# All weight products 256 columns wide, with each streamed operand 192 bytes past its stationary one modulo 256

## What is computed

```python
# first block: ff1, mixer (stick-breaking attention and a gated MLP), ff2
x = x + 0.5 * (silu(h @ w_gate) * (h @ w_up)) @ w_down          # h = rmsnorm(x), width 2816
proj = h @ w_in                                                  # 1024 -> 7168
merged = g_a * (y_a @ w_branch_a) + g_b * (y_b @ w_branch_b)
x = x + merged @ w_out
x = x + 0.5 * (silu(h @ w_gate) * (h @ w_up)) @ w_down
# second block: MoBA layer, then FoX layer, each followed by a squared-ReLU MLP of width 4096
h = h + attention(rms_norm(h) @ w_qkv) @ w_o
h = h + square(relu(rms_norm(h) @ w_up)) @ w_down
```

## Time and profile before

| | |
|---|---|
| median of three runs | 1222.33 us |
| profiled execution | 1222.73 us, its span 1221.0 us |
| PE busy / weight loads | 1209.9 us (99%) / 1033.0 us (85%), 6823 each |
| VectorE busy | 851.5 us (70%) |
| ScalarE busy | 627.8 us (51%) |
| DMA | 221.74 MB, 182 GB/s over the span |
| granted TensorE clock | 0.998 of full |

### The profile page before, as it was taken

The page is one execution under the profiler, slowest core; times in us unless marked ns, Lnnn a source line. Parts: engine busy times, 40 slices in busy tenths (PEclk is TensorE's granted clock), DMA queues, the critical chain, the costliest instruction groups (busy, mean ns, idle before and its releaser), DMA issues.

```text
span 1221.0 us, 17603 instructions
## 1 busy us (share of the span) xinstructions
PE 1209.9 (99%) x6823; PEld 1033.0 (85%) x6823; DVE 851.5 (70%) x1309; ACT 627.8 (51%) x965; POOL 90.2 (7%) x192
## 2 busy tenths in 40 slices
PE   9999999999999999999999999999999999999998
PEld 8788888898888888888888988888888888888886
DVE  6877767576575668777776767865756676876754
ACT  6544446566544446444456665544447465744443
POOL 2000000121000010000003210000000540000000
PEclk9999999999999999999999999999999999999999
DMA  7766666545754555655565445866553654676640
GB/s 235 226 195 199 196 196 192 177 137 161 253 199 146 173 156 183 220 179 185 193 199 171 125 143 183 275 191 191 189 171 110 176 165 156 208 249 192 192 141 35
DMA packets 174899, 221.74 MB, mean 182 GB/s; under 512 B 9268, under 2 KB 103568, under 8 KB 174816
## 3 DMA queue, kind: packets, MB, share of 16 engines
q1 hardware_dynamic: 173264, 217.09, 56.2%
q0 software_dynamic: 1248, 3.00, 0.9%
q10 hardware_dynamic: 304, 0.53, 0.1%
HBM read 219.52 MB, written 1.06 MB: 181 GB/s over the span
## 4 chain that ended last, share of the span: by engine, by line
PE 96%; DVE 1%; DMA 1%; ACT 1%; issue 0%; SPq 0%; DVEq 0%; ACTq 0%
PE bank L1478 56%; PE bank L1565 22%; PE bank L1572 11%; PE bank L1499 1%; PE bank L1738 1%; PE bank L1721 1%; DMA raw<-in_ff_w_up 1%; PE bank L1698 1%; PE bank L1696 1%; PE bank L1712 0%; DVE w_lo L980 0%; PE bank L1742 0%; PE bank L1689 0%; DVE work L1034 0%; PE bank L1930 0%
## 5 line engine op out<-in xcount | busy, mean ns | idle before, releaser
L980 DVE TENSOR_TENSOR w_lo<-raw,w_hi 128x1024 fp32r<-128x1024 f32 (+1 forms) x448 | 490.9, 1119 | 199.2 <-ACT w_hi L628 198.9
L628 ACT ACTIVATE w_hi<-raw 128x1024 fp32r<-128x1024 f32 (+1 forms) x448 | 422.2, 972 | 274.4 <-PE bank L1572 137.1
L1565 PE MATMUL bank<-xt,w_hi 128*128 128x512 f32 x1216 | 320.8, 396 | 2.7 <-DVE work L1034 1.9
L1565 PEld LDWEIGHTS bank<-xt,w_hi 128*128 128x128 f32 x1216 | 213.9, 188 | 40.6 <-DVE work L1034 1.8
L1572 PEld LDWEIGHTS bank<-xt,w_lo 128*128 128x128 f32 x1216 | 167.6, 188 | 16.9
L1572 PE MATMUL bank<-xt,w_lo 128*128 128x256 f32 x1216 | 170.1, 278 | 0.0
L1478 PE MATMUL bank<-w_hi,xt 128*128 128x512 f32 x512 | 160.7, 395 | 0.0
L1478 PE MATMUL bank<-w_hi,yt_lo 128*128 128x512 f32 x336 | 132.6, 395 | 0.0
L1478 PE MATMUL bank<-w_lo,yt_hi 128*128 128x512 f32 x336 | 131.1, 390 | 0.0
L1478 PE MATMUL bank<-w_hi,yt_hi 128*128 128x512 f32 x336 | 131.1, 390 | 0.0
L1478 PEld LDWEIGHTS bank<-w_hi,xt 128*128 128x128 f32 x512 | 95.0, 188 | 21.9 <-issue 2.1
(11 more groups left out here) (212 smaller groups left out, 1164.6 us busy)
## 6 DMA issues: line engine op xcount, KB each, us to landing
raw<-in_w_up SPq DMA_DIRECT2D x64, 512.0 KB, 4.2
raw<-in_w_down SPq DMA_DIRECT2D x64, 512.0 KB, 4.5
raw<-in_w_in SPq DMA_DIRECT2D x56, 512.0 KB, 4.7
raw<-in_ff_w_gate SPq DMA_DIRECT2D x88, 256.0 KB, 3.7
raw<-in_ff_w_up SPq DMA_DIRECT2D x88, 256.0 KB, 4.7
raw<-in_ff_w_down SPq DMA_DIRECT2D x88, 256.0 KB, 5.1
raw<-in_moba_w_qkv SPq DMA_DIRECT2D x24, 512.0 KB, 3.9
raw<-in_w_o SPq DMA_DIRECT2D x16, 512.0 KB, 3.7
```

Source lines behind the costliest of these rows:

```text
L628: act.activation(w_hi[:, c % RING, 0:w], raw[:, c % RAW, 0:w], ACT.Copy).then_inc(s["hi_ready"], 1)
L980: dve.tensor_tensor(w_lo[:, c % RING, 0:w], raw[:, c % RAW, 0:w], w_hi[:, c % RING, 0:w].bitcast(F32), ALU.subtract).then_inc(s["lo_ready" ...
L1565: ins = pe.matmul(up_banks(m)[q][:], w_h[:, k % 2, q * P:(q + 1) * P], flat(xt[:, k, :, :]), start=k == 0, stop=False, skip_group_check=True)
```

## The change

Every weight product is made of matmuls 256 columns wide.
- `three` stays for `project`; the others call `three_halves`, which does the left 256 columns of the bank in three matmuls and then the right 256.
- `high` becomes two matmuls of 256, both into the 256 columns where `low` adds too. The sum of the two halves is so made in PSUM: the reduction L1034 goes, and a chunk of `up` needs two banks instead of four. The gated phases multiply straight from PSUM; the MLP phases take max(g, 0) from PSUM and multiply it with g from PSUM.
- `high` and `low` alternate q by q, except for the first units of a phase, where all of `high` still comes before the wait for `w_lo`.
- The banks of `up` alternate: 0 and 1 for chunk 0, then 4 and 5, then 6 and 7. PE waits at the start of a chunk for what VectorE took of the chunk two before.
- Addresses: `w_hi` and `w_lo` get rows of 1088 instead of 1024 elements, and a unit lies at offset 0 or 32 elements (128 bytes) in its place (`HOME`); `gap_out` grows to 128 bytes and a `gap_end` of 192 bytes follows `ht_lo`. Units streamed past `xt` lie at 128. By sizes modulo 256, `xt` is 192 past the weights, and `yt` and `ht` are 64 past them; so each streamed operand is 192 past its stationary one.
- To make room, `ntri` and `nones` lie in `rbc`, `wst` in `row_gain`, and the load of `row_gain` (broadcast of `final_norm`) moves on SyncE's queue from the first attention to just ahead of the units of `w_out`, behind a wait for `smix_ready`. `small_turns` waits for `const_done` 8 instead of 6.

```diff
+PITCH = WIDE + 64
+BESIDE = 32
...
+        if name in ("stick", "moba", "fox"):
+            homes += [BESIDE] * 4 + [0] * 2 + [BESIDE] * 4 + [0] * (n - 10)
+        else:
+            homes += [BESIDE if name in ("a_in", "gates", "branch_a") else 0] * n
...
-        w_hi = sb("w_hi", [P, RING, WIDE], F32R)
-        w_lo = sb("w_lo", [P, RING, WIDE], F32R)
+        w_hi = sb("w_hi", [P, RING, PITCH], F32R)
+        w_lo = sb("w_lo", [P, RING, PITCH], F32R)
...
-        gap_out = sb("gap_out", [P, 16])
+        gap_out = sb("gap_out", [P, 32])
...
+        gap_end = sb("gap_end", [P, 48])
...
-            return bank[0:4] if m == 0 else up_bank
+            first = 0 if m == 0 else 4 if m % 2 else 6
+            return bank[first:first + 2]
+
+        def up_place(m, q):
+
+            return up_banks(m)[q // 2][:, (q % 2) * S:(q % 2 + 1) * S]
...
-                if n == 6:
-                    sp.dma_start(row_gain[:], final_norm.rearrange("(a n) -> a n", a=1).broadcast_to([P, D]))\
-                        .then_inc(s["gain_in2"], 16)
...
+            sp.wait_ge(s["smix_ready"], TOK * GROUPS // 2)
+            sp.dma_start(row_gain[:], final_norm.rearrange("(a n) -> a n", a=1).broadcast_to([P, D]))\
+                .then_inc(s["gain_in2"], 16)
             proj_units("w_out", wout, lambda i: 0)
...
-                act.activation(w_hi[:, c % RING, 0:w], raw[:, c % RAW, 0:w], ACT.Copy).then_inc(s["hi_ready"], 1)
+                act.activation(w_hi[:, c % RING, o:o + w], raw[:, c % RAW, 0:w], ACT.Copy).then_inc(s["hi_ready"], 1)
...
-                        dve.tensor_reduce(work[0][:, q // 2, (q % 2) * S:(q % 2 + 1) * S],
-                                          up_banks(m)[q][:].rearrange("p (a b) -> p b a", a=2), AX_X, ALU.add)\
-                            .then_inc(s["g_done"], 1)
...
+                        g = up_banks(m)[t][:]
+                        if gated:
...
                             dve.tensor_tensor(work[1][:, t, :].rearrange("p (a b) -> p a b", a=2),
-                                              work[0][:, q // 2, :].rearrange("p (a b) -> p a b", a=2),
+                                              g.rearrange("p (a b) -> p a b", a=2),
                                               rbc[:].unsqueeze(1).broadcast_to([P, 2, S]), ALU.mult)\
                                 .then_inc(s["nrm_done"], 1)
+                        else:
+
+                            dve.tensor_scalar(work[0][:, t, :], g, 0.0, None, ALU.max).then_inc(s["g_done"], 1)
+                            dve.wait_ge(s["g_done"], at(phase, "g_done") + 2 * m + t + 1)
+                            dve.tensor_tensor(work[1][:, t, :], g, work[0][:, t, :], ALU.mult)\
+                                .then_inc(s["h_done"], 1)
...
+            def three_halves(dst, a, b, first, last):
+
+                for half in (slice(0, S), slice(S, 2 * S)):
+                    for n, (p, q) in enumerate(((a[1], b[0]), (a[0], b[0]), (a[0], b[1]))):
+                        ins = pe.matmul(dst[:, half], p, q[:, half], start=first and n == 0 and half.start == 0,
+                                        stop=last and n == 2, skip_group_check=True)
+                return ins
...
+                        if j == 0 and m > 2:
+
+                            pe.wait_ge(s[taken], at(phase, taken) + 2 * m - 2)
...
-                                ins = pe.matmul(up_banks(m)[q][:], w_h[:, k % 2, q * P:(q + 1) * P],
-                                                flat(xt[:, k, :, :]), start=k == 0, stop=False,
-                                                skip_group_check=True)
-                            return ins
+                                w = w_h[:, k % 2, q * P:(q + 1) * P]
+                                pe.matmul(up_place(m, q), w, xt_hi[:, k, :], start=k == 0 and q % 2 == 0, stop=False,
+                                          skip_group_check=True)
+                                pe.matmul(up_place(m, q), w, xt_lo[:, k, :], start=False, stop=False,
+                                          skip_group_check=True)
...
                             for q in range(4):
-                                ins = high(q) if q % 2 == 0 else low(q)
-                                ins = low(q) if q % 2 == 0 else high(q)
-                                if q < 3:
+                                high(q)
+                                ins = low(q)
+                                if j == 3 and q == 1:
                                     ins.then_inc(s["up_done"], 1)
```

More of the change, by code:

```diff
@@ L132, with unit_homes @@
 UNIT = unit_shapes()
+def unit_homes():
+    homes = []
+    for name, adds in PHASES:
+        n = adds.get("units", 0)
+        if name in ("stick", "moba", "fox"):
+            homes += [BESIDE] * 4 + [0] * 2 + [BESIDE] * 4 + [0] * (n - 10)
+        else:
+            homes += [BESIDE if name in ("a_in", "gates", "branch_a") else 0] * n
+    assert len(homes) == UNITS
+    return homes
+HOME = unit_homes()
 def landed_value(c, i):
@@ L201, in two_blocks @@
         gates = sb("gates", [P, TOK, 2 * D], scope=one)
-        wst = sb("wst", [P, GROUPS, P], scope=one)
+        wst = row_gain[:, 0:GROUPS * P].rearrange("p (g t) -> p g t", g=GROUPS)
         bn6 = sb("bn6", [P, TOK * GROUPS, 6], scope=one)
@@ L977, in lo @@
                     return
-                w = UNIT[c][0]
+                w, o = UNIT[c][0], HOME[c]
                 dve.wait_ge(s["hi_ready"], c + 1 + RING * i)
-                dve.tensor_tensor(w_lo[:, c % RING, 0:w], raw[:, c % RAW, 0:w],
-                                  w_hi[:, c % RING, 0:w].bitcast(F32), ALU.subtract).then_inc(s["lo_ready"], 1)
+                dve.tensor_tensor(w_lo[:, c % RING, o:o + w], raw[:, c % RAW, 0:w],
+                                  w_hi[:, c % RING, o:o + w].bitcast(F32), ALU.subtract).then_inc(s["lo_ready"], 1)
             def root(phase, dst=rstd):
@@ L1479, in three @@
                 return ins
+            def three_halves(dst, a, b, first, last):
[4 more added lines that the diff above has]
+                return ins
             def slot(c, k, w):
-                return [buf[:, c % RING, 0:w].rearrange("p (k n) -> p k n", k=k) for buf in (w_hi, w_lo)]
+                o = HOME[c]
+                return [buf[:, c % RING, o:o + w].rearrange("p (k n) -> p k n", k=k) for buf in (w_hi, w_lo)]
             def part(pairs, k, cols):
@@ L1520, in rows_times @@
                         for tok in range(TOK):
-                            ins = three(banks[tok][:], part(src, k, tok_cols(tok)), [v[:, k % 2, :] for v in w],
+                            ins = three_halves(banks[tok][:], part(src, k, tok_cols(tok)), [v[:, k % 2, :] for v in w],
                                         k == 0, k == KT - 1)
@@ L1540, in ffn @@
                 b, gated = at(phase, "units"), phase in ("ff1", "ff2")
+                taken = "nrm_done" if gated else "h_done"
                 tiles_in = 2 if gated else 4
@@ L1554, in up @@
                             first_wait(j)
+                        if j == 0 and m > 2:
+                            pe.wait_ge(s[taken], at(phase, taken) + 2 * m - 2)
+                        if j == 0 and m == 2 and gated:
+                            pe.wait_ge(s["rbc_done"], at(phase, "rbc_done") + 1)
                         w_h, w_l = slot(c + j, 2, 1024)
                         def high(q):
-                            if j == 0 and m == 1 and q == 3 and gated:
-                                pe.wait_ge(s["rbc_done"], at(phase, "rbc_done") + 1)
@@ L1600, in unit @@
                                 row = (j % 2) * 2 + k
-                                ins = three(bank[2 * half + tok][:], part(h_buffers(m), row, tok_cols(tok)),
+                                ins = three_halves(bank[2 * half + tok][:], part(h_buffers(m), row, tok_cols(tok)),
                                             [v[:, k, :] for v in w], False, row == 3)
@@ L1859, in out_unit @@
                     for tok in range(TOK):
-                        ins = three(bank[4 * e + tok][:], part(YT, k, tok_cols(tok)), [v[:, k % 2, :] for v in w],
+                        ins = three_halves(bank[4 * e + tok][:], part(YT, k, tok_cols(tok)), [v[:, k % 2, :] for v in w],
                                     k == 0, k == KT - 1)
```

46 lines of the change are left out of this document (17 added, 29 removed).

## The result

The changed kernel takes 1228.23 us (median of five runs, 1228.13 to 1229.69) against 1222.33 us (1221.72 to 1224.09) of the kernel before in the same session. The ratio is 1.0048, with a 95% interval of 1.0036 to 1.006: slower by half a per cent, where 1209.0 us (1204 to 1217) was forecast.

A forecast was written before the change was run, and what follows sets the result against it. PE was taken as the bound, busy 1209.9 of 1221.0 us. Savings of 8.4 + 0.8 + 2.0 + 0.3 (other products past `yt`) + 2.0 = 13.5 us off 1222.73 gave 1209.2, stated as 1209.0 us, range 1204 to 1217.

The forecast's parts named there:

- The pace after the change: All weight products: 256-wide matmuls at distance 192 would run steadily at 113.3 ns each, as read from attention projections.
- rival 1: Products streaming a weight run slower at 256 wide because operand roles matter; at 118 ns, 1232 us in total; chance 7%.
- `up` 11.10 to 10.88: `up` of each of 38 chunks falls from 11.10 to 10.88 us, 8.4 us saved.
- `down` 0.8 us saved: `down` takes 5.44 instead of 5.46 us 22 times and 10.88 instead of 10.90 us 16 times.
- Products past `xt` 2.0 us saved: 768 products in `a_in`, `gates`, `branch_a` and attention values gain at most 3.5 ns each; 2.0 us taken.
- Stall in ff1: PE's waits in ff1 for the reduction that frees a bank vanish, 2.0 us saved, at least 0.6.
- VectorE: VectorE's busy time falls by about 80 us to about 770 us, the gain hidden by PE.
- What was costed at nothing: Later `h`, PE's new waits before `up` and the moved `row_gain` load are hidden and add 0 us.
- Rival 3: The split helps but pace averages 113.9 ns after disturbances, and half the ff1 stall stays; 1214.5 us; chance 17%.
- rival 2: Each cut of a matmul costs a fixed piece, 3.6 ns, 13 us over 3664 cuts; 1222 us, no change; chance 2%.

The follow-up runs named there:

- e4_break_down: The changed kernel with the first three products of each `down` 512 wide; 1230.23 us, ratio 1.0061.
- e1_up_only: The new 256-wide `up` with VectorE's shorter work, but the old addresses and products that stream a weight 512 wide; 1226.75 us, ratio 1.0034.
- e12: Kernel of e6 with the units streamed past `xt` moved from distance 64 to 0; 1215.48 us, ratio 0.9941.
- e5: Kernel of e1_up_only with an unrelated 128-wide transposition ahead of each chunk's `up` but a phase's first; 1223.0 us, ratio 1.0001.
- e7: The changed kernel with an unrelated 128-wide transposition ahead of each `down` but a phase's first; 1233.04 us, ratio 1.0085.
- e9: The changed kernel with an unrelated 128-wide transposition ahead of each `down` and each `up` but a phase's first; 1245.55 us, ratio 1.0188.
- e3: The changed kernel with its addresses kept, but products that stream a weight 512 wide, at distance 192; 1231.64 us, ratio 1.0071.
- e10: Kernel of e1_up_only with the last but one tile of `down` cut to 256 wide, three 512-wide matmuls before `up`; 1229.39 us, ratio 1.0056.
- e2: The changed kernel, all products 256 wide, with the old addresses (distance 0 past `yt` and `ht`, 64 past `xt`); 1236.85 us, ratio 1.0114.
- e6: Kernel of e1_up_only with the last tile of `down`, except in a phase's last chunk, as six 256-wide matmuls; 1215.58 us, ratio 0.9942.
- e11: Kernel of e6 with only the very last matmul of `down` cut into two of 256 columns; 1215.08 us, ratio 0.9938.
- e8: The kernel before without `gap_in` and `gap_out`, so `xt` is 0 past its weights while `xq` keeps 192; 1228.49 us, ratio 1.005.

## Why the prediction was wrong

**The step that failed** is the one under "The pace after the change": "I take 113.3 ns as the steady pace." There are two steady paces. The 4896 matmuls with a streamed weight ran mostly at 117.8. The prediction had read the 120 and 117 ns at a projection's start as settling; they were the entry, and behind the values, 512 wide and 64 past, it led to the fast pace in 5 of 5 cases. That was luck of what stood ahead: runs with another entry keep the other pace.

The slow pace was in the trace of before, in the chain that was read for `up` and `down`. Four projections of the first attention, 48 matmuls of one kind each:

```profile
241.73 5.85 PE bank L1478 x48
250.53 5.85 PE bank L1478 x48
259.32 5.66 PE bank L1478 x48
267.93 5.64 PE bank L1478 x48
```

Two of them take 0.2 us more than the others, 4 ns per matmul, from start to end. The earlier trace rows shows one of the 5.64 kind. A line of 5.85 would have made 117.8 a pace that can last, and rival 1 much more than 7%.

Point by point:
- `up` 11.10 to 10.88: right where it follows a slow `down` (10.90). Over all, 5.6 of 8.4 us came: behind transpositions of `x`, the first 24 matmuls of ff1, 24 later ones there, 72 of ff2 and nearly two whole `up` of each MLP are slow.
- `down` 0.8 us saved: wrong in sign. The products past `yt` and `ht` lost 11.1 us together.
- Products past `xt` 2.0 us saved: wrong in sign, 2.6 lost, since `a_in` and `gates` ran at 118.
- Stall in ff1: right, a little low. The waits fell by 2.9 us, 2.0 was forecast.
- VectorE: 785.4 us, not about 770. 66 us went instead of 80, of which 8 because the busy time of the reductions was 96.1 us and not count times mean. It bore on nothing.
- What was costed at nothing (later `h`, the new waits, the moved load) did cost nothing: no wait names them.
- Rival 1 had `down` right (11.3 us) and its time nearly (1232) and the wrong cause: `w_out`, e4_break_down and e1_up_only show both paces in both roles. Rival 3 had the mechanism half, "every change of kind disturbs the pace", but took it for a short loss, not for one kept over 96 matmuls.

The Trainium skill (TensorE: Matmul & The Clock Gate, Step-by-step: what each phase is for) says that a weight load steals no read bandwidth from the running matmul. By that no distance could matter, and the runs disagree: 512 columns take 227.1 ns at 0, 230 at 64 and 233 at 192, with e12 moving one group of products from 64 to 0. The formula of the prediction's rival 2 is given in the Trainium skill (TensorE: Matmul & The Clock Gate, Back-to-back issue gap) for an isolated matmul; for streams of loads and matmuls the section has about 131 ns at 512 columns. No trace here comes near that: 512 columns take some 227 ns at best.

**What stays open** is why an entry leads to one pace or the other. By the start times in mlp1 of the changed kernel, the next weight load starts 2 to 4 ns behind a matmul's start in both paces; the matmul behind it starts 110 ns later in the fast one and 114 to 115 in the slow one. That fits two stable phases between the streams of loads and of operands, but no run changed that phase directly. Why an odd matmul turns some entries only (e5, e7, e9) stays open too, and so does the alternation in e3: it goes with the buffer ahead (`ht` or `yt`), with the banks of `up` and with the pace of the chunk before, and no run parts these. So does a `down` that is fast and 256 wide in front of a fast `up`: no kernel here had it. It would bring little, since 512 columns at distance 0 take 227.1 ns anyway. For the products past `xt` no run changed the entry at 192; that it made `a_in` and `gates` slow is argued from the other runs, not shown.

## What to carry to other kernels

A pace read from one stretch holds for that stretch: before a change is priced by it, look at every run of the same kind in the trace, and at what stands ahead of each. Where PE is the bound and has no waits, compare the chain's pieces of equal count; two values that differ by a few per cent and hold to the end are two states, and the last matmul ahead of the run is the cheapest place to change them. The part of a change that gains (`up`, 256 wide) and the part that loses (rows cut in two) should be timed apart: here the first alone lost too, until its entry was mended.

## What the runs showed of the hardware that was not expected

- Runs of 256-wide float32r matmuls, each with its own weight load, hold 113.3 or 117.8 ns for up to some hundreds of matmuls (672 at 118.1 with short waits in between), at a granted clock of 0.998 to 1.0 of full.
- At distance 192 the entry can decide for the whole run: `up` behind 512-wide rows at distance 0 was slow in 60 of 60 entries (e1, e10; so were 5 of 5 projections of e12), behind 256-wide rows at distance 0 fast in 120 of 120 (e2, e6, e11, e12), with two such matmuls as with six or 96. Behind 512-wide rows at 192 it was slow in 16 of 30 (e3).
- The distance between streamed and stationary operand modulo 256 bytes costs 512-wide matmuls 0 to 6 ns (best at 0), and the slow pace of 256-wide ones 2 ns (best, of 0 and 192, at 192).
- 256-wide runs at distance 0 had no fast pace: 120 ns in 53 of 53 runs (e2) and in 17 of 17 (e8), while in e8 the products past `xq`, at 192, took 113 to 115 in the same trace.
